# Where the four weight sums of a seven-product pair are made, and from which pair on an FFN uses seven products

## What is computed

```python
def rmsnorm(x, w):
    y = xf * lax.rsqrt(jnp.mean(xf * xf, axis=-1, keepdims=True) + EPS)
    return (y * w.astype(jnp.float32)).astype(x.dtype)
def swiglu(x, w_gate, w_up, w_down):
    return (jax.nn.silu(x @ w_gate) * (x @ w_up)) @ w_down
```

## Time and profile before

| | us |
|---|---|
| median of 3 runs | 2196.25 (2195.11 to 2198.82) |
| profiled execution, first to last instruction | 2198.8 |

### The profile page before, as it was taken

One profiled execution on the slowest core, in us unless ns is written; L12 is line 12 of the kernel. 1 busy time (PEld: TensorE's weight loads), 2 busy tenths in 40 slices (PEclk: granted clock), 3 DMA queues, 4 the chain that ended last, 5 costly groups with the idle time before them and its releaser, 6 DMA issues.

```text
span 2198.8 us, 40702 instructions
## 1 busy us (share of the span) xinstructions
PE 2160.5 (98%) x16360; PEld 2137.4 (97%) x16360; DVE 1555.5 (71%) x2379; ACT 951.1 (43%) x1495; POOL 45.7 (2%) x50
## 2 busy tenths in 40 slices
PE   7999999999999999999999999999999999999997
PEld 7999999999999999999999999999999899999997
DVE  6898657685555798848679984863776457988485
ACT  5435435454433444515445452544322434445252
POOL 0000000001100000000000000000011100000000
PEclk9999999999999999999999999999999999999999
DMA  5222322224332232222323232232122222223222
GB/s 186 68 88 95 115 67 86 96 82 137 99 118 85 68 102 82 95 87 89 104 70 94 86 96 96 82 101 94 44 96 84 97 77 84 90 87 104 77 86 73
DMA packets 72578, 201.58 MB, mean 92 GB/s; under 512 B 7268, under 2 KB 26980, under 8 KB 72448
## 3 DMA queue, kind: packets, MB, share of 16 engines
q1 hardware_dynamic: 72448, 199.80, 28.1%
HBM read 187.82 MB, written 11.95 MB: 91 GB/s over the span
## 4 chain that ended last, share of the span: by engine, by line
PE 91%; DVE 5%; ACT 2%; issue 1%; DMA 0%; POOL 0%; SPq 0%; DVEq 0%; POOLq 0%
PE ps L479 48%; PE ps L536 32%; PE ps L753 4%; PE ps L608 1%; DVE w_lo L1768 1%; PE ps L784 1%; PE ps L773 1%; PE ps L787 0%; DVE w_lo L1753 0%; PE ps L803 0%; PE ps L617 0%; PE ps L796 0%; PE ps L631 0%; PE ps L797 0%; DMA x<-in_x 0%
## 5 line engine op out<-in xcount | busy, mean ns | idle before, releaser
L479 PE MATMUL ps<-h_lo,w_hi 128*128 128x288 f32 x1616 | 347.0, 294 | 4.1 <-DVE h_hi L2267 4.1
L479 PE MATMUL ps<-h_hi,w_hi 128*128 128x288 f32 x1616 | 346.5, 294 | 0.7 <-DVE w_lo L1753 0.7
L536 PE MATMUL ps<-th_hi,w_hi 128*128 128x288 f32 x1088 | 320.2, 294 | 2.4 <-ACT scratch L1219 2.4
L536 PE MATMUL ps<-th_lo,w_hi 128*128 128x288 f32 x1088 | 320.9, 295 | 0.0
L536 PE MATMUL ps<-th_hi,w_lo 128*128 128x288 f32 x1088 | 319.8, 294 | 0.0
L479 PE MATMUL ps<-h_hi,w_lo 128*128 128x288 f32 x1360 | 290.2, 292 | 0.0
L479 PE MATMUL ps<-xn_hi,w_hi 128*128 128x288 f32 x1152 | 257.2, 300 | 11.6 <-DVE w_lo L1753 8.9
L479 PEld LDWEIGHTS ps<-h_lo,w_hi 128*128 128x128 f32 x1616 | 259.9, 188 | 4.8 <-DVE h_hi L2267 4.5
L479 PEld LDWEIGHTS ps<-h_hi,w_hi 128*128 128x128 f32 x1616 | 259.9, 188 | 1.0 <-DVE w_lo L1753 0.9
L1753 DVE TENSOR_TENSOR w_lo<-raw,w_hi 128x1024 fp32r<-128x1024 f32 x196 | 232.2, 1221 | 36.9 <-ACT w_hi L1185 35.1
L479 PE MATMUL ps<-xn_hi,w_lo 128*128 128x288 f32 x1152 | 251.9, 296 | 0.0
(11 more groups left out here) (288 smaller groups left out, 4119.7 us busy)
## 6 DMA issues: line engine op xcount, KB each, us to landing
raw<-in_w_gate SPq DMA_DIRECT2D x88, 512.0 KB, 3.4
raw<-in_w_up SPq DMA_DIRECT2D x88, 512.0 KB, 4.2
raw<-in_w_down SPq DMA_DIRECT2D x64, 512.0 KB, 3.6
raw<-in_w_mix SPq DMA_DIRECT2D x64, 512.0 KB, 4.2
raw<-in_w_down SPq DMA_DIRECT2D x32, 384.0 KB, 3.2
state_s<-in_state_c SPq DMA_DIRECT2D x4, 1024.0 KB, 7.5
out_c_s<-state_s SPq DMA_DIRECT2D x4, 1024.0 KB, 4.6
state_s<-in_state_g SPq DMA_DIRECT2D x4, 1024.0 KB, 6.1
```

What stands on the lines that cost most here:

```text
L479: ins = nc.tensor.matmul(o, a, b[:, c] if c is not None else b, start=first and j == 0, stop=last and j == 2)
L536: ins = nc.tensor.matmul(ps[:, bank, FIRST], left, b_, start=first and k == 0 and j == 0, stop=k == KT_X // 2 - 1 and j == 2, skip_group_c ...
```

## The change

The weight arrays of gate and up become one, `w_gu`, in which each hidden tile has four units of 128 x 512 side by side: W12, W11 (gate), W21, W22 (up). The signs of the scheme change so that two sums are W21 + W22 (S1) and W11 + W21 (S3), and the other two are S2 = S1 + W11 and S4 = S2 + W12; the hidden tile comes out negated and the down product is added with -0.5.

- SP loads W12 and W11 into the first slot, W21 and W22 into the second, and W11 once more into a new place ahead of the second slot (`s3_start`, 256 KB). Then one adding DMA, issued by GpSimd (512 KB), adds W21 and W22 onto that place and onto W21: S3 and S1 stand there.
- GpSimd makes S2 and S4 with two additions (`weight_sums`). VectorE's four sums are gone. W12 and W11 are rounded, and their remainder made, in one instruction of 1024 columns.
- The order of products is now W11, S3, S2, W12, S1, W22, S4. Two of the additions of parts go: one copy is written into the bank in which the next product accumulates, and gate and up are read from PSUM.
- In FFN 2, 3 and 4 only pair 0 of group 0 is plain (`PLAIN`). The combinations of the tokens are made in the OUT or D phase before it (`early_even`, `x_ready`).
- The norm of the FFNs: `feed_sums` stands inside pair 0, in banks of the other half, and TensorE waits for `var_ready` ahead of pair 1. ScalarE makes `Ln` from PSUM and `Exp` with -0.5 (`feed_log`, `feed_root`); VectorE's mean and reciprocal are gone there. The mixers' norms keep the old form.
- The first pair of each D phase but the last one does its second block bank by bank.
- `bc`, two rows of the mixers, lies inside `raw` now; `s3_start` waits for the mixer's end in FFN 2 and 4.

```diff
+PLAIN = (5, 1, 1, 1)
...
             for g, (k0, k) in enumerate(GROUPS):
+                skip = 0 if g else PLAIN[ffn]
+                skipped = [(skip + 1 - half) // 2 for half in range(2)]
                 out.append(dict(kind="G", pairs=k, base=pair, ffn=ffn, norm=norm, k=KT_X, k0=k0,
-                                group=g, hidden=hidden, seven=seven - (0 if g else 5), plain=5 * ffn,
-                                scaled=3 * ffn - 5))
-                pair, hidden, seven = pair + k, hidden + k, seven + (k if g else k - 5)
+                                group=g, hidden=hidden, seven=seven - skip, plain=sum(PLAIN[:ffn]), skip=skip,
...
+        W12_AT, W11_AT, S3_AT, S1_AT, W22_AT = 0, UNIT, RAW_UP - UNIT, RAW_UP, RAW_UP + UNIT
+        def raw_unit(half, at):
+            return raw[:, half, at:at + UNIT]
+        def s2(half):
+            return T(8 + half)[:, 0:UNIT]
+        def s4(half):
+            return T(7 - half)[:, 0:UNIT]
...
+            def s3_start(ph, i, half):
+                if ph["group"] == 0 and ph["ffn"] % 2:
+                    sp.wait_ge(psum_free, ph["base"] - 3)
+                m = ph["ffn"] * (D_FF // P) + ph["k0"] + 2 * i + half
+                sp.dma_start(raw_unit(half, S3_AT),
+                             io["w_gu"][bass.ds(m, 1), :, UNIT:2 * UNIT].rearrange("o p n -> p (o n)"))\
+                    .then_inc(s3_full[half], 16)
...
                 if ph["kind"] == "OUT":
                     continue
-                with sp.Fori(1 if j == 0 else 0, ph["pairs"] // 2) as i:
-                    for s in range(4):
-                        load(ph, i, s)
+                if ph["kind"] == "G" and ph["group"] == 0:
+                    for m in range(2 if j == 0 else 0, ph["pairs"]):
+                        for blk in range(2):
+                            load(ph, m // 2, 2 * (m % 2) + blk)
+                        if m >= ph["skip"]:
+                            s3_start(ph, m // 2, m % 2)
+                    continue
+                with sp.Fori(0, ph["pairs"] // 2) as i:
+                    for half in range(2):
+                        for blk in range(2):
+                            load(ph, i, 2 * half + blk)
+                        if ph["kind"] == "G":
+                            s3_start(ph, i, half)
             for c in range(2):
                 for m in range(KT_X):
...
+                                feed_sums(ph["norm"])
                             out = [(ps[:, 4 * half + 2 * blk + c, 0:HALF_TOK],
...
-                product(1, b, x_tiles(odd, 0), True).then_inc(product_done, 1)
-                pe.wait_ge(unit_lo, 5 * w + 2)
+                product(U_W11, b + 1, x_tiles(even, 0), True).then_inc(product_done, 1)
+                pe.wait_ge(unit_lo, 4 * w + 1)
+                product(U_S3, b + 3, t_tiles(2), True).then_inc(product_done, 1)
+                pe.wait_ge(unit_lo, 4 * w + 2)
                 pe.wait_ge(copy_done, 3 * w + 1)
-                product(2, b + 1, t_tiles(1), False).then_inc(product_done, 1)
-                pe.wait_ge(unit_lo, 5 * w + 3)
-                product(3, b + 2, t_tiles(2), True).then_inc(product_done, 1)
-                pe.wait_ge(unit_lo, 5 * w + 4)
+                product(U_S2, b + 1, t_tiles(1), False).then_inc(product_done, 1)
+                product(U_W12, b, x_tiles(odd, 0), False).then_inc(product_done, 1)
+                pe.wait_ge(unit_lo, 4 * w + 3)
                 pe.wait_ge(copy_done, 3 * w + 2)
-                product(0, b + 1, t_tiles(0), False).then_inc(product_done, 1)
+                product(U_S1, b + 1, t_tiles(0), False).then_inc(product_done, 1)
                 pe.wait_ge(lo_done, 2 * pair + 2)
-                product(1, b + 3, t_tiles(3), True).then_inc(product_done, 1)
-                pe.wait_ge(unit_lo, 5 * w + 5)
+                pe.wait_ge(part_ready, 2 * w + 1)
+                product(U_W22, b + 2, t_tiles(3), False).then_inc(product_done, 1)
+                pe.wait_ge(unit_lo, 4 * w + 4)
                 pe.wait_ge(copy_done, 3 * w + 3)
-                return product(2, b + 1, x_tiles(odd, 1), False)
+                return product(U_S4, b + 1, x_tiles(odd, 1), False)
...
+            def feed_sums(norm):
+                pe.wait_ge(ssq_done, 4 * (norm + 1))
+                if norm == 0:
+                    pe.wait_ge(const_in, CONST_ALL)
+                for c in range(2):
+                    ins = nc.tensor.matmul(ps[:, 5 + 2 * c, FIRST], ones, half_of(T(5), c), start=True, stop=True)
+                ins.then_inc(feed_done, 1)
...
                             pe.wait_ge(psum_free, pair - 1)
-                        ins = seven_pair(ph, i, half) if half in seven else feature_pair(ph, i, half, half in by_bank)
+                        if half in seven:
+                            ins = seven_pair(ph, i, half)
+                        else:
+                            ins = feature_pair(ph, i, half, half in by_bank, first_norm and half == 0)
+                        ins.then_inc(pe_done, 1)
                         if first_norm and half == 0:
-                            ins = token_sums(ph["norm"])
-                        ins.then_inc(pe_done, 1)
-                if consumer:
+                            pe.wait_ge(var_ready, ph["norm"] + 1)
+                if consumer and ph["skip"] > 1:
                     iteration(0, first_norm=True, bank_wait=ph["base"] > 0, by_bank=(1,))
                     iteration(1)
                     iteration(2, seven=(1,))
                     iteration(3, seven=(0, 1))
+                elif consumer:
+                    iteration(0, first_norm=True, seven=(1,))
+                    with pe.Fori(1, ph["pairs"] // 2) as i:
+                        iteration(i, seven=(0, 1))
+                elif ph["kind"] == "D":
+                    iteration(0, by_bank=(0,))
+                    iteration(1)
                 else:
                     with pe.Fori(0, ph["pairs"] // 2) as i:
-                        iteration(i, seven=(0, 1) if ph["kind"] == "G" else ())
...
+            def feed_log(ph):
+                act.wait_ge(feed_done, ph["ffn"] + 1)
+                nc.scalar.activation(cut2(T(7)), ps[:, 5:8:2, FIRST], ACT.Ln, bias=eps, scale=1.0 / D_MODEL)\
+                    .then_inc(var_ready, 1)
+            def feed_root(n):
+                act.wait_ge(var_ready, n + 1)
+                nc.scalar.activation(rstd[:, :], T(7), ACT.Exp, scale=-0.5).then_inc(rstd_ready, 1)
...
+            def early_even(ph, pp):
+                n = 4 * ph["ffn"] + pp
+                if pp:
+                    act.wait_ge(u_sum, n)
+                nc.scalar.activation(T(2), x[:, 2 * pp, :], ACT.Copy,
+                                     scale=norm_w[:, ph["norm"], 2 * pp:2 * pp + 1]).then_inc(even_ready, 1)
...
+                    u_high(ph, 3)
+                    weights_high(ph, 0, 1)
+                    sums_high(ph, 0, 1)
+                    feed_log(ph)
+                    feed_root(ph["norm"])
+                    evac_g(ph, 0, 0, lambda: seven_start(ph, 0, 1))
+                    seven_half(0, 1)
+                    with act.Fori(1, n - 1) as i:
+                        seven_half(i, 0)
+                        seven_half(i, 1)
                 else:
...
+            def x_ready(j, ph, pp):
+                norm = ph["norm"] + 1
+                if pp and feeds(j):
+                    u_high(PHASES[j + 1], pp - 1)
+                act.wait_ge(psum_free, ph["base"] + pp + 1)
+                if norm < N_NORMS - 1:
+                    xn_high(norm, 2 * pp)
+                    xn_high(norm, 2 * pp + 1)
+                squares(norm, pp)
+                if feeds(j):
+                    early_even(PHASES[j + 1], pp)
...
+            def weight_sums(ffn):
+                for ph in PHASES:
+                    if ph["kind"] != "G" or ph["ffn"] != ffn:
+                        continue
+                    for m in range(ph["skip"], ph["pairs"]):
+                        i, half, pair = m // 2, m % 2, ph["base"] + m
+                        pool.wait_ge(raw_full[2 * half + 1], 8 * (pair - half) + 16)
+                        pool.wait_ge(s3_full[half], sums_at(ph, i, half))
+                        G.dma_start(raw[:, half, S3_AT:S1_AT + UNIT], io["w_gu"][ffn * (D_FF // P) + ph["k0"] + m, :,
+                                                                                2 * UNIT:4 * UNIT],
+                                    accum_op=ALU.add).then_inc(sums_full[half], 16)
+                        w = ph["seven"] + m
+                        pool.wait_ge(raw_full[2 * half], 8 * (pair - half) + 16)
+                        pool.wait_ge(sums_full[half], sums_at(ph, i, half))
+                        if ph["group"] == 0 and m == ph["skip"]:
+                            pool.wait_ge(ssq_done, 4 * (ph["norm"] + 1))
+                        if ph["group"] == 0:
+                            if half == 0:
```

(40 more changed lines are left out.)

283 lines of the change are left out of this document (136 added, 147 removed).

## The result

| | before | after |
|---|---|---|
| median of the runs (us) | 2197.46 (4 runs, 2195.11 to 2198.82) | 2207.22 (4 runs, 2205.52 to 2207.53) |
| ratio, 95% interval | | 1.0039 (1.0027 to 1.0052) |
| profiled execution (us) | 2198.8 | 2205.3 |

What follows compares the result with a forecast made beforehand. TensorE was taken as the bound: matmul count times pitch, plus idle time. Terms -20.8 + 2.0 + 5.0 + 5.7 + 1.5 = -6.6 us, from the median 2196.25 to 2189.7 us; overall range 2179 to 2206, the forecast's own 2184 to 2193.

Steps and rivals of the forecast that it cites:

- Fewer matmuls: FFN 2, 3, 4: twelve pairs drop from 96 to 84 matmuls (17.4 us), old beginnings' loss goes (3.4 us): -20.8 us.
- By-bank order: First pair of 11 down phases: matmuls in a row no longer share their left tile, 0.2 us each, +2.0 us.
- FFN 2 and 4: Beginnings behind a mixer's output phase: TensorE waits 1.1 us for the Ln, 1.4 for a copy; 2.5 each, +5.0 us.
- the port rival: At three beginnings S2 takes the shared port from VectorE and the clock falls each time: 2194.4 us; chance 0.2.
- FFN 3: Beginning behind FFN 2's last down phase: VectorE falls behind, Ln late by 1.9 us, copy 1.6 more: +5.7 us.
- FFN 1: Beginning: TensorE idles 4.0 us for the Ln behind pair 0, an earlier wait disappears: +1.5 us net (0 to 4).
- The steady loop: 80 steady pairs: GpSimd's adding DMA, S2, S4 and port blocking take 10.1 us, fit in 11.10, cost nothing.
- All hidden: Rival: second pair's preparation and the Ln are done ahead of TensorE at the beginnings: 2177.4 us; chance 0.13.

Runs made afterwards that it cites:

- w22_early: Changed kernel with reordered beginnings and down phases, adding DMA kept; newly, W22 of the first seven-product pair is rounded and its remainder made earlier: 2187.03 us, ratio 0.9958.

## Why the prediction was wrong, step by step

The step that failed is the price of the beginnings of FFN 2, 3 and 4: the sum has +5.0 and +5.7 us for them, and they cost 11.8 and 10.4. Each was costed as one wait for the Ln and one for a copy, where the runs showed an Ln that is later by 1.6 to 1.7 us more, a lower clock behind it at two of them, and a late round of weights behind that. The down phases failed too, in a smaller way. By the profiled executions the change was to bring -6.6 us and brought +6.5. The 13.1 us between, by the steps of the sum:

- **Fewer matmuls, -20.8.** Right: 144 fewer, and a steady pair of 11.10 us.
- **By-bank order, +2.0.** Wrong in kind. The eight phases of 8 tiles cost 0.27 each, 2.1, and that this is near the size that I gave is luck: the block that I held to be the cost saves 1.0 us, and what costs is the longer pitch up to its end. The last phases of FFN 1 and FFN 3, of 6 tiles, cost 0.93 each, 1.9, where they keep that pitch throughout. That is 2.0 us more than forecast. I read 130 ns as the pitch of a down phase. It is one of two, and every down phase of the new kernel begins with the other, for a reason that stays open; the 133.3 ns of the output phases of the kernel before could have told me that there are two.
- **FFN 2 and 4, +2.5 each.** Measured 5.45 and 6.35 (6.95 removed, stretches shorter by 1.5 and 0.6): 6.8 us more. The 6.35 flatters the change, since the kernel before lost 1.5 us to the clock in the output phase ahead of FFN 4 and the changed one didn't; without that it is 7.9. The Ln was late by 2.83 and 2.84, not 1.1: u_sums lost 1.9 us to S2 and S4, where the forecast had neither and the port rival 1.3. Behind it the clock fell in FFN 4 (the 1.2 GHz level, behind 2.84 us idle), and not in FFN 2 (behind 2.83), as the third last number of these windows shows; I had taken full clock, and the 1.8 us of the rival for a fall is in no row. In FFN 4 it cost some 2.5 us: 28 matmuls in 6.0 us, where 130 ns each make 3.6. What the forecast lacked wholly is the price further behind: the late round over W22, the loads and the adding DMA. The seven pairs behind the Ln took 80.1 us in FFN 2 where 7 x 11.10 = 77.7, 2.4 more, and the forecast had 1.4 for a copy. That the late W22 is in it is shown by w22_early alone, behind other mended waits.
- **FFN 3, +5.7.** Measured 10.45 (6.95 removed, the stretch longer by 3.5), 4.7 more: the Ln late by 3.47 instead of 1.9, a stretch at the 1.2 GHz level (1.6, matmuls every 240 ns instead of 130), 0.9 for the pitch of the down phase ahead, and S4 late in the pairs behind.
- **FFN 1, +1.5.** Right in mechanism, idle 4.10 for a forecast 4.0, with the dip; +0.4 net, since the first seven-product pairs gained 0.8.
- **The steady loop, 0.** GpSimd's sums 1.3 to 1.6 us and 5.7 us for the DMA stand as sized; the mean fits, the tail doesn't: one landing in ten takes 7.5 us or more, and FFN 1's third group lost 1.1 us to one, and the other phases of steady pairs took 0.03 to 0.06 us more each, 0.4 in all. The median price hid the tail.
- The mixers, the start and the end: -0.7, in which is -1.2 of mixer 1, where the kernel before had the stretch of 1635.5 at the low clock.

The two windows of the changed kernel, behind the beginnings of FFN 2 and 4:

```profile
718.00:722.00 4.00, 3.44 (x24) 3.20 (x24) 1.42 (x2) 3.96 (x5) 1.78 (x2) 1.00 0.35 118
1813.50:1819.50 6.00, 6.00 (x28) 6.00 (x28) 3.09 (x4) 5.30 (x8) 2.56 (x2) 0.55 0.18 62
```

The steps together: 2.0 + 6.8 + 4.7 - 1.1 + 1.5 - 0.7 = 13.2, for 13.1. By the medians 3 us more were lost, most of it the clock of the profiled execution before, as said at the result. Of the rivals, the port happened (I gave it 0.2), and at 2194.4 us was too small by all that came behind the Ln. All hidden needed, as I wrote, 1 to 2 us less on ScalarE at each place. The orders up to w22_early find them, and it was still not enough: that kernel is at 2187.0, not 2177.4.

A range of 2179 to 2206 left 2207.2 out because its costs were summed as if each beginning had one last wait. There were up to four one behind another (Ln, the copies of products 1 and 3, W22), and each run above took one away and met the next.

## What to carry to other kernels

Where an engine prepares the next stage ahead of a wait, list in its order everything behind the wait that someone needs for the stage after, loads of a slot included; the time that a beginning loses first shows one or two rounds later, when a loop with little slack catches up. Order an in-order engine's list by when each input is there and not by the program's logic: Ln, W, copies and W22 moved, with nothing else changed, were worth some 16 us here, GpSimd's later wait included. Take a DMA's price in a loop from its tail, not its median, and keep GpSimd's additions out of chains of short dependent VectorE operations.

## What the hardware showed that I had not expected

- Matmuls in twos run at 130.0 or 133.3 ns at the same granted clock of 1.00, and keep what they have for hundreds of matmuls; a run of single-bank matmuls of the right length changes it. Over a down phase of 384 this is 1.28 us. What sets it at the start of a phase stays open.
- A DMA of 512 KB that adds onto SBUF lands after 5.7 us (5.2 to 9.6), the same without the add after 4.2 (3.4 to 5.8).
- A short VectorE operation that meets GpSimd's addition takes 0.9 to 1.0 us longer (0.45 becomes 1.43), each time anew; beside long remainders in the steady pairs it cost TensorE nothing, even with four additions a pair.
- Three changes between Ln, Exp and Silu cost three table loads of 1.28 us, with the next operation 0.02 us behind each (715.92 + 1.28, Ln at 717.22). The Trainium skill (ScalarE: Activation LUTs, What ACT_TABLE_LOAD costs) gives 2.66 us with a drain; no drain shows here, and the measurement decides.
- Behind idle times of 2.84 and 3.47 us the granted clock fell, behind one of 2.83 it stayed at 1.00, and in the kernel before it fell behind 1.9 and 2.06: the length of the idle time alone doesn't tell it.

```profile
715.92 1.28 ACT L1375 ACT_TABLE_LOAD   x1
717.22 0.74 ACT L1375 ACTIVATE scratch<-ps,rstd_eps 128x576 f32<-128x576 f32 x1
717.98 1.28 ACT L1381 ACT_TABLE_LOAD   x1
```
